# A two-layer hybrid decoder on one core: layers and expert bodies written out, one copy of the gathered tokens, a ninth weight buffer, norms applied by tile

## The chip, the core and the metric

The kernel runs on 1 of the cores of one Trainium2 chip. The metric is the device time of one execution in microseconds. The median of three runs of the kernel before is 1702.33 us (1701.65 to 1702.81).

## What is computed

The reference takes 256 tokens of 1024 float32 features through two layers. Each layer has three sub-layers, and each ends in x <- LayerNorm(alpha * x + f(x)).

```python
for l in range(2):
    mix = parallel_mixer(x, ...)      # short convolution and latent attention, gated, projected
    x = layer_norm(ALPHA * x + mix, ln1_g[l], ln1_b[l])
    xat = memory_cross_attention(x, mem, ...)          # 4 heads into 256 memory tokens
    x = layer_norm(ALPHA * x + xat, ln2_g[l], ln2_b[l])
    ffn = moe_ffn(x, ...)             # 64 experts, top 8 in 4 of 8 groups, plus a shared expert
    x = layer_norm(ALPHA * x + ffn, ln3_g[l], ln3_b[l])
```

An expert is silu(x @ w_gate) * (x @ w_up), times the token's gate, @ w_down, with inner width 256. Every expert's weights, 3 MB in float32, are read in every layer.

## The kernel before, in words

**Engines and order.** Each engine has its own program, written by hand, with semaphores between them. SyncE (SP) issues every weight load in one queue, in order; `alone` (L316) makes it wait for one semaphore and then go on, so what is behind a wait in its program waits too. TensorE, VectorE (DVE), ScalarE (ACT) and GpSimd (POOL) each run a loop `Fori(0, DEPTH)` over the two layers (L598, L769, L1201, L1479), with the counts they wait for worked out in registers from the layer and from `base`, the number of expert bodies already run. Only SyncE has the layers written out (L487).

**Dense part.** A layer has 24 weight loads of up to 2 MB (`LOADS`, L94), which go round the six slots of `ring`. Projections run as jobs through four PSUM banks `work` (L70 to L90). The layer begins with `xk0`, half of the projection of the memory tokens, then transposes XN (`xT0`) into XT with gain and bias of the norm applied on the way, then `cq`, `ckv`, `c`, `h` and so on. Only the transposed copy has gain and bias by then; X, in rows, is needed for the residual sum and gets them separately: GpSimd multiplies and adds for norms 1 and 2 (L627 to L638), both tiles of 128 tokens one after the other, once both are normalized, and then counts `ln_applied`. The gains and biases in rows are in `gb`, loaded by `load_ln` (L466).

**Norm 3.** The sum of the experts stands in the four PSUM banks `moe_sum`. `add_and_normalize(l, None, 2)` (L1392) takes statistics of both tiles, then multiplies the centred sums by the gain (`centred`, L1441), which needs `gb`, and then writes X (L1452). ScalarE writes XN (L1185); for tile 1 it waits for `centred_ready`, that is for the `centred` of tile 1 and so for the load. SyncE issues that load of ln3 for layer 0 behind the first six dense loads of layer 1 (L501 to L503), since `gb` shares its place with `xg_second`.

**Routing.** After norm 2, VectorE picks groups and experts in a chain of some 60 small instructions (L1637 to L1703), computes how many rounds of 32 slots the busiest expert needs (L1705 to L1713), and builds `sel`, the one-hot matrices of 8 experts (L1718). TensorE then gathers tokens as matmuls with `sel`, in a high and a low part: ScalarE rounds X to `x_hi` (L1299), GpSimd subtracts to get `x_lo` (L643). Before that TensorE does the shared expert's eight down products into `moe_sum` (L975) and counts `shared_down`, on which SyncE's load of unit 5 waits.

**Experts.** They run in 32 pairs of two. A pair has three units of 2 MB: expert 0's gate and up, expert 1's gate and up (for pairs "in halves", L372, the first and second half of both), and both down matrices. Units 0 to 7 lie in the six ring slots and two places of the arena (`ahead`, L237). Eight pairs are a body (24 units, so each place is used three times), and four bodies are a layer. SyncE loads unit m as soon as unit m - 8 has been read (`wait_unit_read`, L477): a down unit is free when the pair's down products are done, a gate and up unit when both are done, or its half for pairs in halves (the first three pairs of a layer, and the eighth of each body). On TensorE body 0 is written out (L1119) and bodies 1 to 3 are a loop (L1122 to L1124); SyncE has the same; ScalarE and VectorE loop over all four. Within a pair TensorE does gate and up (L1076), half of the previous pair's scatter into `moe_sum`, one gather matmul group for the next four pairs, the transposes of `hid`, the other half of the scatter, down (L1107) and another gather. Gathered tokens of one batch of four pairs lie in `xg_first`, those of the next in `xg_second` and `xg_more`.

## Time and profile before

| | us |
|---|---|
| median of three runs | 1702.33 |
| lowest and highest | 1701.65, 1702.81 |
| the profiled execution, time | 1701.95 |
| the profiled execution, first to last instruction (span) | 1700.1 |
| mean granted TensorE clock | 0.986 of full speed |
| busy: TensorE matmul, weight load | 1627.4, 907.1 |
| busy: VectorE, ScalarE, GpSimd | 430.8, 284.5, 71.0 |
| read from HBM | 507.64 MB, 299 GB/s over the span |

Times in the trace are counted from the span's start, and all reasoning is made on the profiled execution. Layer 0's experts run from about 384 to 842 us, layer 1's from about 1228 to 1687. Matmuls are pipelined, so a busy TensorE may still not be at its peak; the idle time in brackets behind a row, and what ended it, is what tells of a wait. "issue" there is a wait for nothing that the profile shows. SPq is SyncE's own queue; its rows are the times at which loads are issued, not those at which they land.

### The profile page before, as it was taken

What the parts mean: (1) busy time and instruction counts of PE and PEld (TensorE: products, weight loads), DVE (VectorE), ACT (ScalarE), POOL (GpSimd) and SP (SyncE); (2) the same over time, 40 slices, a digit from 0 to 9 for tenths busy, and PEclk for the clock granted to TensorE, in tenths of its full rate; (3) what the DMA queues carried; (4) which work ended last, traced back from release to release, by engine and by line L of the source; (5) the groups of instructions that cost most, each with busy time, mean ns of one, the idle gap of its engine ahead of it and who ended that gap; (6) DMA issues with size and microseconds to landing.
All of it is one profiled execution on the core that took longest, in us unless ns stands there. A gap on an engine that the chain in (4) does not pass through costs nothing.

```text
span 1700.1 us, 20631 instructions
## 1 busy us (share of the span) xinstructions
PE 1627.4 (96%) x8037; PEld 907.1 (53%) x8038; DVE 430.8 (25%) x893; ACT 284.5 (17%) x560; POOL 71.0 (4%) x88
## 2 busy tenths in 40 slices
PE   7999999999999999999789999999999999999996
PEld 5878867573333333333368787765733333333332
DVE  2122221162222222212222312112622222222223
ACT  1022011131111111111110320111311111111111
POOL 1000020030000000000000000200300000000000
PEclk9999999999999999999989999999999999999998
DMA  9246442468999999999950554434699999999995
GB/s 347 71 160 237 164 158 106 148 247 355 412 421 421 418 422 422 419 422 422 399 187 18 218 188 163 149 138 146 218 411 413 421 421 418 422 421 419 422 422 206
DMA packets 111222, 509.66 MB, mean 300 GB/s; under 512 B 8354, under 2 KB 12580, under 8 KB 68660
## 3 DMA queue, kind: packets, MB, share of 16 engines
q1 hardware_dynamic: 110592, 508.59, 75.2%
q8 instruction: 48, 0.79, 0.2%
q0 software_dynamic: 224, 0.12, 0.1%
q14 instruction: 18, 0.15, 0.0%
q10 hardware_dynamic: 340, 0.02, 0.0%
HBM read 507.64 MB, written 1.05 MB: 299 GB/s over the span
## 4 chain that ended last, share of the span: by engine, by line
PE 76%; DMA 11%; SPq 8%; DVE 3%; issue 1%; ACT 1%; DVEq 0%; ACTq 0%
PE work L686 37%; PE work L1076 20%; DMA ring<-in_w_up 9%; PE work L1107 9%; SPq L521 5%; PE work L987 3%; PE moe_sum L1030 3%; SPq L498 2%; DMA ring<-in_w_xk 1%; DMA arena<-in_ln_b 1%; PE work L1094 1%; PE moe_sum L1022 1%; PE work L994 0%; PE work L819 0%; DVE busiest L1708 0%
## 5 line engine op out<-in xcount | busy, mean ns | idle before, releaser
L1076 PE MATMUL work<-ring,arena 128*64 128x512 f32 x1216 | 288.6, 599 | 19.8 <-DMA ring<-in_w_up 13.6
L686 PE MATMUL work<-XT,ring 128*128 128x256 f32 (+1 forms) x1408 | 280.3, 360 | 1.3 <-DVE arena L1570 1.3
L686 PEld LDWEIGHTS work<-XT,ring 128*128 128x128 f32 x1408 | 247.5, 190 | 32.6 <-issue 3.0
L1076 PEld LDWEIGHTS work<-ring,arena 128*64 128x64 f32 x1216 | 90.1, 137 | 168.7 <-issue 156.7
L1107 PE MATMUL work<-ring,hidden 128*64 128x512 f32 x768 | 175.4, 598 | 1.0 <-DVE hidden L1769 1.0
L1776 DVE TENSOR_TENSOR out_lo<-work,out_hi 128x512 fp32r<-128x512 f32 x128 | 88.6, 692 | 231.1 <-ACT out_hi L1332 231.1
L686 PE MATMUL work<-ring,arena 128*128 128x512 f32 (+1 forms) x336 | 140.4, 577 | 0.0
L1765 DVE SCALAR_TENSOR_TENSOR hidden<-hidden,slot_gate,work 128x256 f32<-128x256 f32 x64 | 30.7, 480 | 419.1 <-ACT hidden L1328 419.1
L1332 ACT CAST out_hi<-work 128x512 fp32r<-128x512 f32 x128 | 75.1, 587 | 213.6 <-PE work L1107 213.6
L1328 ACT ACTIVATE hidden<-work 128x256 f32<-128x256 f32 x64 | 24.6, 385 | 491.7 <-PE work L1076 491.7
L1107 PEld LDWEIGHTS work<-ring,hidden 128*64 128x64 f32 x768 | 50.9, 136 | 100.4 <-issue 85.2
L686 PEld LDWEIGHTS work<-ring,arena 128*128 128x128 f32 x336 | 63.7, 190 | 71.7 <-issue 65.1
L987 PE MATMUL work<-sel,x_hi 128*128 128x256 f32 x288 | 91.7, 339 | 4.1 <-DVE sel L1718 3.7
L987 PEld LDWEIGHTS work<-sel,x_hi 128*128 128x128 f32 x288 | 55.7, 193 | 70.2 <-issue 63.2
L1076 PE MATMUL work<-arena 128*64 128x512 f32 x320 | 85.9, 596 | 7.1 <-DMA ring<-in_w_up 5.0
L1076 PE MATMUL work<-ring,xg_more 128*64 128x512 f32 x320 | 86.6, 592 | 0.0
L987 PE MATMUL work<-sel,x_lo 128*128 128x256 f32 x288 | 77.7, 291 | 0.0
L596 POOL TENSOR_TENSOR small<-small,minus_half 128x1 f32<-128x1 f32 x20 | 11.2, 559 | 1457.2 <-DVE small L1420 1454.4
L686 PE MATMUL work<-memT,ring 128*128 128x256 f32 x256 | 60.8, 402 | 10.1 <-issue 7.0
L1030 PE MATMUL moe_sum<-out_hi,selT 32*128 32x512 f32 x512 | 64.5, 494 | 1.8 <-DVE out_lo L1776 1.6
L686 PEld LDWEIGHTS work<-memT,ring 128*128 128x128 f32 x256 | 51.8, 203 | 19.3 <-issue 11.6
L1107 PE MATMUL work<-arena,hidden 128*64 128x512 f32 x256 | 58.5, 598 | 0.0
(227 smaller groups left out, 1424.7 us busy)
## 6 DMA issues: line engine op xcount, KB each, us to landing
ring<-in_w_gate SPq DMA_DIRECT2D x96, 1024.0 KB, 18.1
ring<-in_w_up SPq DMA_DIRECT2D x96, 1024.0 KB, 20.9
ring<-in_w_down SPq DMA_DIRECT2D x96, 1024.0 KB, 17.4
arena<-in_w_gate SPq DMA_DIRECT2D x32, 1024.0 KB, 20.5
arena<-in_w_up SPq DMA_DIRECT2D x32, 1024.0 KB, 22.3
arena<-in_w_down SPq DMA_DIRECT2D x32, 1024.0 KB, 17.8
ring<-in_w_in SPq DMA_DIRECT2D x28, 1024.0 KB, 12.7
ring<-in_w_xk SPq DMA_DIRECT2D x8, 1024.0 KB, 8.3
```

The lines of the kernel that those rows point to most:

```text
L498: sp.dma_start(dst, src).then_inc(slot_loaded[s], 16)
L521: sp.dma_start(dst, src).then_inc(slot_loaded[u], 16)
L686: mm = pe.matmul(dst, a, b, start=(k == 0), stop=(k == len(pairs) - 1))
L987: mm = pe.matmul(dst[:, :, t, :], part[:, t, c * P:(c + 1) * P], src, start=(part is x_hi), stop=(part is x_lo))
L1022: pe.matmul(moe_sum[i][:, :].rearrange("p (q c) -> p q c", c=KC), ident_r[:, :], rows, start=False, stop=False, skip_group_check=True)
L1030: mm = pe.matmul(moe_sum[2 * (q % TT) + half][:, :], selT[rows, b, k, :], part[rows, half * BANK:(half + 1) * BANK], start=False, stop=Fal ...
L1076: mm = pe.matmul(work[0][rows, :], xg[b][c][:, k * P + e * TT * SLOTS:k * P + (e + 1) * TT * SLOTS], w, start=(c == 0), stop=(c == KC - 1))
L1107: mm = pe.matmul(w[rows, :], hidT[:, c, rows], wd[:, e, c, half * BANK:(half + 1) * BANK], start=(c == 0), stop=(c == 1))
L1328: act.activation(hid, work[0][:, 0:EXPERT_DIM], ACT.Silu).then_inc(silu_ready, 1)
L1332: act.copy(out_hi[:, half * BANK:(half + 1) * BANK], work[1 + half][:, :]).then_inc(hi_ready[half], 1)
L1765: dve.scalar_tensor_tensor(out=hid, in0=hid, scalar=slot_gate[:, b, k:k + 1], in1=work[0][:, EXPERT_DIM:2 * EXPERT_DIM], op0=ALU.mult, op1 ...
L1776: dve.tensor_tensor(out_lo[:, cols], work[1 + half][:, :], out_hi[:, cols].bitcast(F32), ALU.subtract).then_inc(lo_ready[half], 1)
```

## The change

- The layer loops of all engines are written out, so layer 0's counts are constants. On TensorE and SyncE bodies 1 and 2 are written out too (only body 3 stays in the loop, with further rounds).
- `xg` is one buffer; the second batch of a body is kept in it in permuted blocks, so that it takes the blocks that the first batch has given up. `xg_more` goes. The room becomes `KEYS` (the cross-attention keys), and keys and `gb` together are a ninth unit, `EXTRA`. It holds unit 8 of each layer's first body and is used once a layer; its first half is loaded after the cross-attention scores, its second after norm 2 is applied.
- After that, places go round the old eight again (`place_of`), and the units wait for other predecessors (`wait_unit_read`).
- GpSimd applies norms by tile, and norm 3 of layer 0 too. ScalarE writes XN of layer 0's norm 3 without waiting for the gain; VectorE's `centred` steps stay only in layer 1, for tile 0.
- `load_ln` of ln3 is issued at the end of a layer's expert loads, ahead of the next layer's dense ones.
- `x_hi` is rounded by tile, `x_lo` follows, four of the shared expert's eight down products move in among the gathers, and the count of rounds moves behind the gathers.

```diff
+EXTRA = UNITS
...
-        xg_first, xg_second = view(2 * K, KC, BATCH * P), view(0, KC // 2, BATCH * P)
-        xg = [[xg_first[:, c, :] for c in range(KC)],
-              [(xg_second if c < KC // 2 else xg_more)[:, c % (KC // 2), :] for c in range(KC)]]
+        xg = view(2 * K, KC, BATCH, P)
+        def gathered(b, c):
+            return xg[:, c, :, :] if b == 0 else xg[:, c % 2::2, c // 2, :]
+        def gathered_pair(b, c, k):
+            return xg[:, c, k, :] if b == 0 else xg[:, 2 * k + c % 2, c // 2, :]
         ahead = view(6 * K, UNITS - RING, SLOT)
-        unit = [ring[:, u, :] if u < RING else ahead[:, u - RING, :] for u in range(UNITS)]
+        unit = [ring[:, u, :] if u < RING else ahead[:, u - RING, :] for u in range(UNITS)] + [arena[:, 0:SLOT]]
...
+        def place_of(m, first=False):
+            if not first:
+                return m % UNITS, m // UNITS + 1
+            return (m, 1) if m <= UNITS else ((m - UNITS - 1) % UNITS, (m - UNITS - 1) // UNITS + 2)
+        def units_used(u, l, body, first=False):
+            n = body * RING_USES
+            if u < RING:
+                return n + (l + 1) * DENSE_USES
+            if u == UNITS - 1:
+                return n + DEPTH - (l if first else l + 1)
+            return l if u == EXTRA else n
...
-            def wait_unit_read(m, pairs, halves, first=False):
-                q, part = divmod(m - UNITS, 3)
+            def wait_unit_read(m, pairs, halves, first=False, second=False):
+                if first:
+                    prev = m - UNITS - 1 if m <= 2 * UNITS else m - UNITS
+                elif second and m < UNITS:
+                    prev = m - (UNITS - 1) if m < UNITS - 1 else m - 2 * UNITS + 1
+                else:
+                    prev = m - UNITS
+                q, part = divmod(prev, 3)
                 if part == 2:
-                    alone(sp, down_filled[1], pairs + (q + 1))
+                    alone(sp, down_filled[1], snap(sp, pairs + (q + 1)))
                 else:
-                    alone(sp, gate_up_done, halves + (2 * q + (part if in_halves(q % BODY_PAIRS, first) else 1) + 1))
+                    late = part if in_halves(q % BODY_PAIRS, first or (second and q < 0)) else 1
+                    alone(sp, gate_up_done, snap(sp, halves + (2 * q + late + 1)))
...
-                    if l > 0 and n == RING - 1:
-                        alone(sp, gate_up_done, snap((base + 1) * (2 * BODY_PAIRS)))
-                        load_ln(l - 1, ln3_g, ln3_b, 2)
...
+                b, n = job("xscores", X_HEADS - 1)
+                alone(sp, filled[b], l * BANK_USES[b] + n)
+                load_unit(EXTRA, first[EXTRA // 3], True, (0,))
...
+                alone(sp, ln_applied, l * 3 + 3)
+                load_unit(EXTRA, first[EXTRA // 3], True, (1,))
...
+                load_body(base, first, range(EXTRA + 1, UNITS * RING_USES), True)
+                load_body(base + 1, firsts(1), range(UNITS * RING_USES), second=True)
+                load_body(base + 2, firsts(2), range(UNITS * RING_USES))
                 sp.reg_mov(more, 1)
-                sp.reg_mov(start, 1)
+                sp.reg_mov(start, 3)
...
+                alone(sp, down_filled[1], snap(sp, (base + 1) * BODY_PAIRS + (EXTRA // 3 + 1)))
+                load_ln(l, ln3_g, ln3_b, 2)
...
+                def root(which, t):
+                    alone(pool, moments_ready, l * 6 + (2 * which + t + 1))
+                    inverse_root(ln_rstd[:, t:t + 1], moments[:, 2 * t + 1:2 * t + 2], ln_rstd_ready)
+                def apply_norm(which, t):
+                    for half in range(2):
+                        pool.wait_ge(norm_ready[half], l * 6 + (2 * which + t + 3))
+                    pool.wait_ge(ln_loaded, (l * 3 + which + 1) * 32)
+                    step(pool.tensor_tensor(X[:, t, :], XN[:, t, :], gb[:, 0, :], ALU.mult))
+                    settle()
+                    ins = pool.tensor_tensor(X[:, t, :], X[:, t, :], gb[:, 1, :], ALU.add)
+                    if t == TT - 1:
+                        ins.then_inc(ln_applied, 1)
+                    elif which == 1:
+                        ins.then_inc(first_applied, 1)
+                    else:
+                        step(ins)
+                for which in range(2):
                     for t in range(TT):
+                        root(which, t)
+                        apply_norm(which, t)
+                for t in range(TT):
+                    pool.wait_ge(x_hi_ready, l * TT + (t + 1))
+                    pool.tensor_tensor(by_chunk(x_lo, t), in_chunks(X, t), by_chunk(x_hi, t).bitcast(F32),
+                                       ALU.subtract).then_inc(x_split_ready, 1)
+                for t in range(TT):
+                    root(2, t)
+                if l < DEPTH - 1:
                     for t in range(TT):
+                        apply_norm(2, t)
...
-            with pe.Fori(0, DEPTH) as l:
-                base = pe.value_load(bodies[0:1, bass.ds(l, 1)], min_val=0, max_val=4 * BODIES * DEPTH)
-                uses = pe.snap(base * RING_USES + l * DENSE_USES)
+            done = 0
+            for l in range(DEPTH):
+                base = done
+                seen.clear()
...
+                def add_shared(t, half, c):
+                    if half == 0 and c == 0:
+                        wait_job(l, "shared", t)
+                    return pe.matmul(moe_sum[2 * t + half][:, :], sharedT[:, c, t * P:(t + 1) * P],
+                                     w_down_sb[:, c, half * BANK:(half + 1) * BANK],
+                                     start=(c == 0), stop=False, skip_group_check=True)
+                shared_products = [(t, half, c) for t in range(TT) for half in range(2) for c in range(2)]
+                for t, half, c in shared_products[0:4]:
+                    add_shared(t, half, c)
...
+                    if c % 2 == 0:
+                        mm = add_shared(*shared_products[4 + c // 2])
+                        if c == KC - 2:
+                            mm.then_inc(shared_down, 1)
...
+                expert_body(snap(pe, base + 1))
+                expert_body(snap(pe, base + 2))
                 pe.reg_mov(more, 1)
-                pe.reg_mov(start, 1)
+                pe.reg_mov(start, 3)
...
-                        if t == 1:
-                            act.wait_ge(centred_ready, l + 1)
...
+                def round_input(t):
+                    act.copy(by_chunk(x_hi, t), in_chunks(X, t)).then_inc(x_hi_ready, 1)
+                normalize(l, 1, (0,))
+                tile_transposed(l, "xT2", 1, 0)
+                normalize(l, 1, (1,))
+                act.wait_ge(first_applied, l + 1)
+                round_input(0)
+                tile_transposed(l, "xT2", 1, 1)
                 w = wait_filled(act, l, "router")
                 take(act.activation(score, w[:, 0:TT * P].rearrange("p (t e) -> p t e", t=TT)[:, :, 0:EXPERTS], ACT.Sigmoid),
                      l, "router")
                 for t in range(TT):
+                    if t == 1:
+                        act.wait_ge(ln_applied, l * 3 + 3)
+                        round_input(1)
...
+                if l < DEPTH - 1:
+                    shift(0)
+                    shift(1)
+                    return
                 dve.wait_ge(ln_loaded, (l * 3 + 3) * 32)
                 settle()
-                for t in (1, 0):
-                    if t == 0:
-                        for half in range(2):
-                            dve.wait_ge(norm_ready[half], l * 6 + 7)
-                    for half in range(2):
-                        cols = slice(half * BANK, (half + 1) * BANK)
-                        ins = dve.scalar_tensor_tensor(out=centred[:, t, cols], in0=moe_sum[2 * t + half][:, :],
-                                                       scalar=moments[:, 2 * t:2 * t + 1], in1=gb[:, 0, cols],
-                                                       op0=ALU.subtract, op1=ALU.mult)
-                        if t == 1 and half == 1:
-                            tell(ins, centred_ready, l + 1)
-                            shift(1)
-                        else:
-                            step(ins)
+                for half in range(2):
+                    cols = slice(half * BANK, (half + 1) * BANK)
+                    step(dve.scalar_tensor_tensor(out=centred[:, cols], in0=moe_sum[half][:, :],
+                                                  scalar=moments[:, 0:1], in1=gb[:, 0, cols],
+                                                  op0=ALU.subtract, op1=ALU.mult))
+                shift(0)
+                shift(1)
                 settle()
-                for t in range(TT):
-                    dve.wait_ge(ln_rstd_ready, l * 6 + (5 + t))
-                    tell(dve.scalar_tensor_tensor(out=X[:, t, :], in0=centred[:, t, :], scalar=ln_rstd[:, t:t + 1],
-                                                  in1=gb[:, 1, :], op0=ALU.mult, op1=ALU.add),
-                         (layer_done if t == 0 else ln_applied), (l + 1 if t == 0 else l * 3 + 4))
+                tell(dve.scalar_tensor_tensor(out=X[:, 0, :], in0=centred, scalar=ln_rstd[:, 0:1],
+                                              in1=gb[:, 1, :], op0=ALU.mult, op1=ALU.add), layer_done, 1)
+                for half in range(2):
+                    cols = slice(half * BANK, (half + 1) * BANK)
+                    dve.wait_ge(norm_ready[half], l * 6 + 7)
+                    step(dve.tensor_tensor(X[:, 1, cols], XN[:, 1, cols], gb[:, 0, cols], ALU.mult))
+                settle()
+                tell(dve.tensor_tensor(X[:, 1, :], X[:, 1, :], gb[:, 1, :], ALU.add), ln_applied, l * 3 + 4)
...
+                then(dve.tensor_scalar(busiest[:, 1:2], busiest[:, 0:1], float(SLOTS), 1.0, ALU.is_gt, ALU.add))
+                for n in range(2, P // SLOTS):
+                    then(dve.tensor_scalar(busiest[:, 2:3], busiest[:, 0:1], float(n * SLOTS), None, ALU.is_gt))
+                    then(dve.tensor_tensor(busiest[:, 1:2], busiest[:, 1:2], busiest[:, 2:3], ALU.add))
+                step(dve.tensor_copy(rounds[:, l:l + 1], busiest[0:1, 1:2]))
+                then(dve.tensor_copy(bodies_f[:, 0:1], bodies[:, l:l + 1]))
+                then(dve.scalar_tensor_tensor(out=bodies_f[:, 1:2], in0=busiest[0:1, 1:2], scalar=float(BODIES),
+                                              in1=bodies_f[:, 0:1], op0=ALU.mult, op1=ALU.add))
+                tell(dve.tensor_copy(bodies[:, l + 1:l + 2], bodies_f[:, 1:2]), routing_ready, l + 1)
```

## Rows read from the trace of the kernel before

**Rows 1.** The page, 40 equal slices of the span: transfer rate.

```profile
GB/s 347 71 160 237 164 158 106 148 247 355 412 421 421 418 422 422 419 422 422 399 187 18 218 188 163 149 138 146 218 411 413 421 421 418 422 421 419 422 422 206
```

**Rows 2.** Windows: us, busy PE, PEld, DVE, ACT, POOL, clock, DMA share, GB/s.

```profile
420.00:500.00 80.00, 79.81 (x426) 30.33 (x420) 20.14 (x36) 13.08 (x25) 0.00 (x0) 1.00 1.01 416
...
450.00:460.00 10.00, 10.00 (x46) 3.27 (x42) 1.98 (x3) 1.11 (x2) 0.00 (x0) 1.00 0.99 390
...
845.00:850.00 5.00, 1.16 (x3) 0.99 (x4) 0.94 (x4) 1.45 (x2) 0.56 (x1) 0.50 1.05 384
```

**Rows 3.** Timeline of SyncE in the first body: start us, us, what.

```profile
387.79 0.80 SPq L521 DMA_DIRECT2D ring<-in_w_down  x2
...
432.32 0.80 SPq L521 DMA_DIRECT2D ring<-in_w_down  x2
...
475.17 0.81 SPq L521 DMA_DIRECT2D ring<-in_w_down  x2
```

**Rows 4.** L521, issue to landing, loads issued at 387.8 and 388.2.

```profile
DMA to landing us min/median/max: 4.8/5.8/6.9
```

**Rows 5.** The same, of those issued last at 418.5, 432.7 and 466.9.

```profile
DMA to landing us min/median/max: 10.6/11.7/12.7
...
DMA to landing us min/median/max: 6.4/7.4/8.5
...
DMA to landing us min/median/max: 13.1/14.6/16.1
```

**Rows 6.** Timeline of TensorE, first gate and up that waits for weights.

```profile
677.11 0.64 PE L1076 MATMUL work<-arena 128*64 128x512 f32 x1 [1.25 <-DMA ring<-in_w_up]
```

**Rows 7.** Timeline of TensorE, from layer 0 to layer 1.

```profile
848.84 16.04 PE L686 MATMUL work<-memT,ring 128*128 128x256 f32 x64 [7.00 <-issue]
868.97 1.20 PE L734 MATMUL work<-ident,arena 128*128 128x128 f32 x8 [4.10 <-ACT arena L1185]
...
876.21 18.99 PE L686 MATMUL work<-ring,XT 128*128 128x384 f32 x60 [0.85 <-DVE XT L1461]
```

**Rows 8.** Timeline of VectorE, from layer 0 to layer 1.

```profile
865.91 1.41 DVE L1441 SCALAR_TENSOR_TENSOR arena<-moe_sum,small,arena 128x512 f32<-128x512 f32 x2 [19.91 <-DMA arena<-in_ln_b]
...
874.83 0.18 DVE L1481 COPY par<-par_all 128x17 f32 x1 [3.60 <-issue]
```

**Rows 9.** L498, issue to landing, w_xk loads issued at 816.3 and 816.8.

```profile
DMA to landing us min/median/max: 17.6/19.0/20.4
```

**Rows 10.** Timeline of SyncE, from layer 0 to layer 1.

```profile
852.01 2.61 SPq L470 DMA_DIRECT2D arena<-in_ln_g  x1
```

**Rows 11.** The chain that ended last, first dense stages of both layers.

```profile
31.25 1.78 PE work L734 x16
33.04 45.85 PE work L686 x192
...
922.83 1.09 PE work L793 x10
```

**Rows 12.** Timeline of GpSimd, routing of layer 0.

```profile
353.14 4.67 POOL L631 TENSOR_TENSOR X<-arena 128x1024 f32<-128x1024 f32 x2 [1.21 <-ACT arena L1189]
357.89 4.80 POOL L634 TENSOR_TENSOR X<-X,arena 128x1024 f32<-128x1024 f32 x2
370.52 5.68 POOL L643 TENSOR_TENSOR x_lo<-X,x_hi 128x1024 fp32r<-128x1024 f32 x2 [7.83 <-ACT x_hi L1299]
```

**Rows 13.** Timeline of VectorE, routing of layer 0.

```profile
370.58 2.82 DVE L1708 TENSOR_TENSOR busiest<-busiest 128x1 f32<-128x1 f32 x1
...
376.51 0.69 DVE L1718 TENSOR_TENSOR sel<-pos,iota 128x512 fp32r<-128x512 f32 x1
```

**Rows 14.** Timeline of TensorE, routing of layer 0.

```profile
368.35 7.03 PE L975 MATMUL moe_sum<-ring,arena 128*128 128x512 f32 x16
377.26 0.39 PE L987 MATMUL work<-sel,x_hi 128*128 128x256 f32 x1 [1.87 <-DVE sel L1718]
...
384.03 7.09 PE L1076 MATMUL work<-ring,arena 128*64 128x512 f32 x32
```

142 lines of the change are left out of this document (51 added, 91 removed).

## Prediction

> **What bounds the kernel now.** I read the slices first: two layers of the same shape, in each a dense part of some 375 us in which DMA has room, then the experts, where the transfer rate stands at about 420 GB/s for some ten slices [rows 1]. The window from 420 to 500 says the same closer up: 416 GB/s at a full DMA share, while TensorE is at its upper clock, 2.4 GHz [rows 2]. A unit is 128 x 4096 floats, 2.10 MB, so at 421 GB/s one takes 4.98 us and the three of a pair 14.9 us. TensorE needs about 13.9 us for a pair: gate and up start at 384.0 [rows 14], and 21 pairs on TensorE is ready at 677.1 - 1.25 = 675.9 [rows 6]. Transfers are the slower side, so the lead that was loaded ahead melts, and from 677.1 on gate and up wait for their weights [rows 6]. The end of each expert part is therefore the landing of the last unit, not TensorE's work.
>
> The second bound is the passage between the layers. TensorE ends the last scatter at 848.84 - 7.00 = 841.8, starts the first projection of layer 1 at 848.8, finishes it at 864.9, and waits again: the transposes come at 869.0 and the first full run of `cq` at 876.2 [rows 7]. Two different things hold it. The 7.0 us ahead of 848.8 are labelled "issue"; the weights are not what is late, since the later of the two `w_xk` loads landed at 816.8 + 20.4 = 837.2 [rows 9]. Then VectorE sits 19.9 us [rows 8] until `ln_b` is there, because the last norm multiplies by it before tile 1 is let go, and after its two X writes another 3.6 us pass at the loop's end before L1481 [rows 8]. `ln_g` was issued only at 852.0, behind six dense loads [rows 10].
>
> Third, the 16 us of routing ahead of the experts, where VectorE's chain ends in `sel` at 376.5 and the first gather starts at 377.3 [rows 13, 14].
>
> **The passage (layers written out, load of ln3 ahead, XN straight from moe_sum).** The change lets ScalarE write XN of both tiles as soon as the shifts are there, without the load, and GpSimd applies gain and bias to X beside it. Removed: the 19.9 us wait, four `centred` instructions, two X writes and the way back to the loop's start. What is late next is the first projection itself. Steps after the last scatter's end E: about 0.5 us to fall through, 15.4 us for the 64 matmuls (it took 16.0 at a lower clock [rows 7]; the clock was 0.50 in the window before [rows 2], and I expect a shorter dip after a shorter idle), then 1.9 us to `cq`, a little over the 1.8 us that layer 0 shows from the start of the transposes at 31.25 to 33.04 [rows 11]. So `cq` at E + 17.8 instead of E + 34.4, that is 16.6 us. The run from there is warmer: 45.85 us in layer 0 against 876.21 to 922.83 = 46.6 in layer 1 [rows 11], 0.7 us more. **Sum 17.3 us.** GpSimd's four operations of 2.4 us each [rows 12] lie beside the projection; if that cover went they would delay only the residual, which is wanted at the mix sum more than 100 us on. The two ln3 loads now stand ahead of `w_xk`: 1 MB, 2.5 us at 421 GB/s, and I allow up to twice that again, since the wait for `ln_b` ended 13.9 us after `ln_g` was issued [rows 8, 10]; `w_xk` lands at 837.2 + 2.5 to 6.0 against a demand at 842.3, so at worst 0.9 us shows. Bounds of the passage: 10.3 us if the 7.0 us stay where they are, 19.5 if the projection runs at the full clock throughout and nothing is lost.
>
> The Trainium skill (Runtime: NRT & Kernel Launch, Instruction fetch mechanics) says that code is fetched ahead only in sequence and that a taken branch to a page not held stalls until it is fetched. By that rule the 7.0 us go, but the way back inside the expert loop would stall too, and writing out bodies would bring more. The trace agrees only with the first: the loop inside goes back near 607 and TensorE keeps its pace there. I give written-out bodies zero: no TensorE wait there names anything, and from pair 21 on the stage is bound by transfers anyway.
>
> **The routing.** Three edits go together. Norm 2 is applied by tile, so GpSimd's four operations (353.1 to 362.7 [rows 12]) become tile 0 in the idle time before and tile 1 at about 353.1 to 358.0; `x_hi` of tile 0 is rounded early, and the `x_lo` subtractions, 2.84 us each [rows 12], move from 370.5 to about 358 and 363.4. The count of rounds leaves the chain ahead of `sel`: eight small instructions, of which one took 2.8 us; from the end of L1703, some 0.7 us ahead of 370.6, to `sel` at 376.5 that is 6.6 us [rows 13]. TensorE puts four of eight shared products (16 matmuls 7.03 us [rows 14], so 3.5 us) in among the gathers.
> But the rows show why one was long: L1708 ended at 373.4 just as the first `x_lo` did, at 370.52 + 2.84 [rows 12, 13]. A VectorE operation with two SBUF inputs stood until GpSimd's was through. Moved to 363.4, the second `x_lo` stands across the group comparisons, which are such operations; I take 2.6 us of its 2.84 as lost there. Then `chosen` comes at 369.3 rather than 366.7, TensorE idles 1.4 us, places, does four products until 373.5; `sel` is there by 373.3. Gathers took 384.0 - 377.3 = 6.8 us [rows 14], in part at the lower clock; with 3.5 us of products among them and a warm clock about 8.9, so gate and up start at 382.4 instead of 384.0. **Gain 1.5 us per layer**, bounds -0.5 (the clock falls again) and +3.5 (no blocking).
> The Trainium skill (SBUF — State Buffer, Who interferes with whom) states this as an exclusive lock held for a whole instruction and counts plain VectorE copies and scalar operations in 2-port modes in as well. By it more of the router's chain would stand and the gain would be near zero; by the row alone it is what I took.
>
> **The ninth buffer.** On its face it lets 2.1 MB more be loaded before the experts start, 5.0 us at 421 GB/s off the end of a stage bound by transfers. I went through who frees what. The unit is used once per layer, so unit m of the first body takes the place of m - 9 only up to 16; from 17 it waits for m - 8 as before, and in the second body units 0 to 6 wait for m - 7, one *less* ahead. Times of before: a load issued into an empty queue at 387.8 landed 6.9 us after its second half's issue at 388.2, 7.4 us after release [rows 3, 4]. Before, unit 8 landed at 395.1 and unit 17, released at 432.3, landed 8.5 us after 432.7, at 441.2 [rows 3, 5]. With the change unit 9 lands at 395.1 and unit 16 as unit 15 did, at 418.5 + 12.7 = 431.2 [rows 5], and the next is not released until gate and up of pair 3 end at 432.2: it lands at 439.6. Of 5.0 us 1.6 are left. Then unit 25: before it was released at 466.3 and landed at 466.9 + 16.1 = 483.0 [rows 5]. Now it waits for unit 18, read when pair 6's gate and up end at 475.1 (the release after which `w_down` was issued at 475.2 [rows 3]), and lands at 482.5. **Gain 0.5 us per layer**; bounds -1.3 (before, 390 GB/s between 450 and 460 [rows 2] delayed unit 25 by about 1.8 us over the even pace; a like dip behind the new waits would come on top) and +1.6. What is behind SP's waits then is the rest of the queue: each bubble moves every later unit.
> The last shared product, and with it the sixth unit's load, comes later by about 5 us; the queue is empty then, and unit 9 is released only 4 us after the start, so this costs nothing.
>
> **The rest.** One copy of the gathered tokens: the same copies and matmuls at other addresses, none added; a block is overwritten after the pair that reads it, in TensorE's own order. Zero; a few tenths if strided copies are slower, hidden under gate and up. End of layer 1: two `centred` instructions (0.7 us each [rows 8]) and an X write are exchanged for two half products and one sum of the same widths; +0.1 us.
>
> **Sum.** 17.3 + 2 x (1.5 + 0.5) - 0.1 = 21.2 us off the profiled execution's 1701.95 (span 1700.1 and 1.85 around it) gives 1680.8; the median is 0.4 above that execution, so **1681 us**.
>
> **Rivals.** *The ninth buffer pays in full* and the router is not blocked: 5.0 instead of 0.5 and up to 3.5 instead of 1.5 per layer; with the first alone 1681 - 9 = 1672. For it speaks that the stage is bound by transfers; against it the release times, which are rules of the code. 0.1. *The passage keeps its issue stall*, because TensorE fetches its next code under a full queue either way: 7 us back, 1688. For it: nothing shows that the branch alone is guilty. Against: the scatter after the inner loop's end started with no such stall. 0.2. *Cold code in the written-out bodies* makes it slower: two more bodies per layer run once each, fetched while transfers are at 420 GB/s; each stall would be of the passage's size, 7.0 us. It decides from four unhidden stalls on, 28 us against the 21 gained, which is 1681 + 28 = 1709; with two in each of the four such bodies it is 1681 + 56 = 1737. Against it: the first body of before ran once, was written out, and shows no stall. 0.03. My forecast 0.6; what is left, 0.07, is mixtures between.
>
> **The numbers.** The range takes the passage at 15 to 19.5, the routing and buffer bounds partly offsetting each other, and reaches to the rival at 1688: 1673 to 1689. A measurement tells about 0.2%, 3.4 us, from no change: faster 0.95, within it 0.02, slower 0.03.
>
> **What would show it.** Right: no wait for `ln_b`; the projection of layer 1 starting within 2 us of the last scatter, `cq` 17 to 19 us after it; `sel` near 373 with a long VectorE instruction in the comparisons; the first gate and up near 382; a hole in the transfer rate near 430 and 473, and the wait for weights beginning about pair 20 as before. Wrong: an "issue" of 7 us at the passage, an unbroken rate from 388 on with the expert part 5 us shorter, or holes in TensorE in the second and third bodies.

## The result, and the profile after

The changed kernel takes **1680.26 us** (median of 4 runs, 1679.52 to 1683.15) against 1701.99 for the kernel before on the same chip: a ratio of 0.9875, 95% interval 0.9862 to 0.9889. The profiled execution has a span of 1677.7 us against 1700.1. Cut at the same five points of TensorE's timeline in both traces, the 22.4 us between the spans lie as follows (us; S is the start of the first gate and up, E the end of the last scatter, cq the first full run behind the transposes):

```
part                              before   after   gained  predicted
layer 0 up to S                   384.0    380.7     3.4     1.5
experts of layer 0, S to E        457.8    460.3    -2.5     0.5
passage, E to cq of layer 1        34.4     15.7    18.7    16.6
layer 1, cq to S                  352.2    348.1     4.1     2.2
experts of layer 1                458.9    460.6    -1.7     0.5
behind the last scatter            12.8     12.4     0.4    -0.1
```

(2.2 is 1.5 for the routing and 0.7 for the warmer run.) The total came out as forecast (1681 us), but two terms were too small, and the expert part, where I forecast a small gain, got longer. The slices still show two layers bound by transfers at 421 GB/s; the page's line:

```profile
GB/s 347 75 149 252 143 156 135 176 226 373 372 407 421 418 421 421 418 421 421 410 301 0 289 162 126 165 142 176 276 385 394 421 421 419 421 421 419 421 421 216
```

**The passage.** TensorE's timeline, where [rows 7] had 7.00 us of issue ahead of the projection and 4.10 behind it:

```profile
839.41 0.50 PE L1082 MATMUL moe_sum<-out_hi,selT 32*128 32x512 f32 x4 [0.82 <-DVE out_lo L1836]
...
840.56 0.40 PE L1082 MATMUL moe_sum<-out_lo,selT 32*128 32x512 f32 x4
840.89 14.08 PE L728 MATMUL work<-memT,ring 128*128 128x256 f32 x64
854.80 1.94 PE L777 MATMUL work<-ident,arena 128*128 128x128 f32 x16
856.66 13.71 PE L728 MATMUL work<-ring,XT 128*128 128x384 f32 x45
```

No gap is left. The projection starts as the scatter ends, and takes 13.9 us (840.89 to 854.80) because the clock never left its upper level (granted clock 1.00 in the stretches from 840 to 850 and from 850 to 860).

**The routing.** VectorE and GpSimd, where [rows 12, 13] had the blocked L1708 and `sel` at 376.5:

```profile
357.69 2.80 DVE L1702 TENSOR_TENSOR arena<-arena,iota 128x64 f32<-128x64 f32 x1
...
363.23 2.87 DVE L1721 TENSOR_TENSOR arena<-small 128x64 f32<-128x64 f32 x1
...
371.93 0.69 DVE L1767 TENSOR_TENSOR sel<-pos,iota 128x512 fp32r<-128x512 f32 x1
```

```profile
357.56 2.86 POOL L680 TENSOR_TENSOR x_lo<-X,x_hi 128x1024 fp32r<-128x1024 f32 x1
363.11 2.91 POOL L680 TENSOR_TENSOR x_lo<-X,x_hi 128x1024 fp32r<-128x1024 f32 x1 [2.70 <-ACT x_hi L1340]
```

Each VectorE instruction of 2.8 us ends within 0.1 us of a GpSimd subtraction (360.49 and 360.42; 366.10 and 366.02). The second stands in the group comparisons, as forecast; the first, on L1702, is one that the forecast didn't have. TensorE gathers from 372.76 and starts gate and up at 380.65: 7.9 us with four shared products among them, where I had 8.9.

**The transfers behind the ninth unit.** Three rows of the table by stretches (engines, granted clock, DMA share, GB/s), then SyncE's issues:

```profile
420.00:430.00 10.00, 9.81 (x56) 4.00 (x53) 2.83 (x6) 1.55 (x3) 0.00 (x0) 1.00 0.78 310
...
450.00:460.00 10.00, 10.00 (x58) 3.87 (x60) 1.68 (x4) 0.97 (x2) 0.00 (x0) 1.00 1.01 358
...
470.00:480.00 10.00, 10.00 (x58) 4.12 (x56) 3.47 (x7) 2.73 (x5) 0.00 (x0) 1.00 0.90 360
```

```profile
414.76 0.33 SPq L548 DMA_DIRECT2D arena<-in_w_gate  x1
415.13 0.43 SPq L548 DMA_DIRECT2D arena<-in_w_up  x1
428.94 0.80 SPq L548 DMA_DIRECT2D ring<-in_w_down  x2
...
463.32 0.42 SPq L548 DMA_DIRECT2D ring<-in_w_up  x1
471.73 0.33 SPq L548 DMA_DIRECT2D ring<-in_w_gate  x1
```

These are the two holes of the forecast: nothing is issued from 415.6 to 428.94 (before, [rows 2] had 416 GB/s from 420 to 500 at a full share), and again from 463.7 to 471.73. The share falls to 0.78 and 0.90, and what had been loaded ahead is mostly spent again.

### The profile page after: what moved, and what is told of

Its sections match the earlier page's. It is cut to its first block, busy times and chain, and to the rows that moved or that the text cites. A ratio compares the mean times of both kernels' runs of the same rounds, so it can differ in the third digit from the quotient of the medians.

```text
span 1677.7 us, 19829 instructions
## 1 busy us (share of the span) xinstructions
PE 1618.2 (96%) x8037; PEld 901.8 (54%) x8037; DVE 423.4 (25%) x886; ACT 280.5 (17%) x555; POOL 80.5 (5%) x92
## 4 chain that ended last, share of the span: by engine, by line
PE 79%; DMA 12%; SPq 5%; DVE 3%; issue 1%; ACT 1%; DVEq 0%
PE work L728 38%; PE work L1128 20%; DMA ring<-in_w_up 11%; PE work L1159 9%; SPq L548 5%; PE moe_sum L1082 3%; PE work L1035 3%; PE moe_sum L1021 1%; DMA ring<-in_w_xk 1%; PE work L1146 1%; PE moe_sum L1074 1%; PE work L1042 0%; PE work L777 0%; PE work L864 0%; DVE arena L1721 0%
## 5 line engine op out<-in xcount | busy, mean ns | idle before, releaser
L1128 PE MATMUL work<-ring,arena 128*64 128x512 f32 x1536 | 365.5, 599 | 19.6 <-DMA ring<-in_w_up 12.4
L1128 PEld LDWEIGHTS work<-ring,arena 128*64 128x64 f32 x1536 | 118.4, 137 | 206.8 <-issue 194.7
L1128 PE MATMUL work<-arena 128*64 128x512 f32 x512 | 136.6, 598 | 10.0 <-DMA ring<-in_w_up 7.4
L1128 PEld LDWEIGHTS work<-arena 128*64 128x64 f32 x512 | 42.4, 137 | 92.4 <-issue 84.5
L1082 PEld LDWEIGHTS moe_sum<-out_hi,selT 32*128 32x128 f32 x512 | 24.5, 181 | 60.8 <-issue 52.3
```

The costliest lines, as they stand in the source:

```text
L1082: mm = pe.matmul(moe_sum[2 * (q % TT) + half][:, :], selT[rows, b, k, :], part[rows, half * BANK:(half + 1) * BANK], start=False, stop=Fal ...
L1128: mm = pe.matmul(work[0][rows, :], gathered_pair(b, c, k)[:, rows], w, start=(c == 0), stop=(c == KC - 1))
```

## The experiments

Each is an edit of the changed kernel. e3 to e7 and e10 ran once each, e1, e2 and e9 four times, e8 and e11 five times; where a kernel ran more than once the time is the median. The cuts above are made in one trace of each (us):

```
run                                   S      experts 0  passage  cq to S  experts 1
before                                384.0  457.8      34.4     352.2    458.9
changed                               380.7  460.3      15.7     348.1    460.6
e1  no ninth unit                     379.5  462.3      15.7     348.1    460.8
e2  ninth unit rotates                379.0  455.4      15.7     348.1    455.5
e3  TensorE's layer loop back         381.0  460.4      25.9     348.0    460.5
e4  XN waits, load late               379.6  461.1      29.5     348.6    460.4
e5  shared products first             382.2  460.2      15.7     349.8    460.3
e6  bodies in the loop                380.5  458.9      15.7     348.1    459.0
e7  XN waits, load early              380.9  460.4      15.7     348.1    461.0
e8  ninth rotates, tables early       380.6  455.1      15.7     347.8    455.6
e9  no ninth, bodies in the loop      379.2  458.8      15.7     348.1    459.7
e10 as e9, shared products first      381.8  458.3      15.7     349.8    459.2
e11 as e8, first subtraction early    378.5  455.7      15.7     347.0    455.8
```

S of layer 0 lies up to 2 us apart in kernels that do the same work up to there (e2 and e7), and SyncE's issues near 310 us are already apart by 1.7 (e2 and the changed kernel); `cq` to S of layer 1 agrees within 0.1 us in six kernels. So sizes of the routing are read in layer 1.

**e1, without the ninth unit.**

```
-            return (m, 1) if m <= UNITS else ((m - UNITS - 1) % UNITS, (m - UNITS - 1) // UNITS + 2)
+            return m % UNITS, m // UNITS + 1
...
-                if first:
-                    prev = m - UNITS - 1 if m <= 2 * UNITS else m - UNITS
-                elif second and m < UNITS:
-                    prev = m - (UNITS - 1) if m < UNITS - 1 else m - 2 * UNITS + 1
-                else:
-                    prev = m - UNITS
+                prev = m - UNITS
```

> The changed kernel with the ninth unit taken out: unit m waits for m - 8 throughout, nothing else differs. Theory A (who frees what decides, and a unit used once a layer costs more at its two seams than it gives): from the first gate and up to the last scatter layer 0 takes 457.8 us and layer 1 458.9 as in the kernel before, against 460.3 and 460.6 in the changed one, no hole in the transfer rate near 420 to 430 and 470 to 480; total some 4 us below the changed kernel, 1676. Theory B (a unit more ahead pays its 5.0 us per layer even if used once): the expert parts grow by about 5 us each, total 1690.

Measured: 1680.35 us (1679.54 to 1681.15, ratio 0.987, interval 0.985 to 0.989), no difference from the changed kernel. The holes are gone: 419 GB/s at a share of 1.01 between 420 and 430. The expert parts take 462.3 and 460.8 us, so by this pair the ninth unit, used once, brings 2.0 and 0.2; in layer 0 this trace has slices of granted clock 0.83 from 720 to 730 and from 790 to 800, which the changed kernel's has not, and one such pair's first half took 8.78 us against 7.09. Both figures of the expectation were missed. The ninth unit is no loss, but as used it is worth little, and the longer expert part is not its doing.

**e2, the ninth unit in rotation for three bodies** (unit m waits for m - 9 up to the end of the third body).

```
+            g = i * UNITS * RING_USES + m
+            return g % (UNITS + 1), g // (UNITS + 1) + 1
...
+                prev = m - UNITS if i is None else m - UNITS - 1
```

> The changed kernel with the ninth unit kept in the round for the three bodies that are written out: unit m goes to place m mod 9 and waits for m - 9 (72 units, eight turns of nine); the fourth body goes round eight. Theory A: no wait of the queue is late any more, so the whole lead of 2.10 MB is kept and each expert part is 5.0 us shorter than with eight units: 452.8 and 453.9 us, 7.5 us less than in the changed kernel; total 1665 to 1668, and an unbroken 420 GB/s from 390 on. Theory B (the lead is lost to something else, such as the halves' smaller rows or TensorE's own pace): expert parts stay within 2 us of the changed kernel's and the total within 4 us of 1680.

Measured: 1669.65 us (1667.97 to 1671.07), ratio 0.981, interval 0.979 to 0.983: faster than the kernel before and, by intervals that don't touch, than the changed one; some 2 us above what theory A gave. The stretch with the first hole is full:

```profile
420.00:430.00 10.00, 9.90 (x58) 3.94 (x60) 2.63 (x6) 1.02 (x3) 0.00 (x0) 1.00 1.01 419
```

and the expert parts take 455.4 and 455.5 us, 4.9 and 5.1 less than the changed kernel's: a unit's transfer is 5.0 us. Against e1, which has no ninth unit, it is 6.9 and 5.3. The same buffer pays in full when the wait distance stays at nine for three bodies, and hardly at all when it falls back to eight in the first. The fourth body of e2 falls back to eight too, and loses nothing: its queue moves 419 to 423 GB/s in every stretch from 700 to 800, and TensorE waits for weights from 713.80 on, so that by then places come free as fast as they are filled.

**e3, TensorE's layer loop back.**

```
-            for l in range(DEPTH):
-                base = done
-                seen.clear()
+            with pe.Fori(0, DEPTH) as l:
+                base = pe.value_load(bodies[0:1, bass.ds(l, 1)], min_val=0, max_val=4 * BODIES * DEPTH)
```

> The changed kernel, with only TensorE's layer loop put back as a loop (the base is read from memory again at its head); loads, norms and bodies as in the changed kernel. Theory A (the 7.0 us of issue are the way back of TensorE's loop): an idle time labelled issue of 6 to 8 us is back between the last scatter of layer 0 and the first projection of layer 1, cq comes about 8 us later than in the changed kernel (a lower clock on top), total 1687 to 1689. Theory B (the stall was due to the full transfer queue or to the wait for the load of the norm): no such stall, total within 2 us of 1680.

Measured: 1689.89 us, span 1688.0, that is 10.3 over the changed kernel's. The timeline:

```profile
840.91 0.40 PE L1079 MATMUL moe_sum<-out_lo,selT 32*128 32x512 f32 x4
849.70 12.54 PE L728 MATMUL work<-memT,ring 128*128 128x256 f32 x49 [8.39 <-issue]
```

8.39 us of issue are back. The projection then takes 15.6 us instead of 13.9; the table by stretches has a granted clock of 0.65 in the idle time and still 0.84 behind it, where the changed kernel has 1.00 in both:

```profile
840.00:850.00 10.00, 1.54 (x17) 0.67 (x14) 3.94 (x13) 2.79 (x4) 3.74 (x4) 0.65 1.06 382
850.00:860.00 10.00, 10.00 (x40) 8.53 (x40) 0.00 (x0) 0.59 (x1) 6.70 (x3) 0.84 1.04 383
```

Of the difference in span 8.4 + 1.7 is all but 0.2. What else rides on the loop (VectorE, ScalarE, SyncE written out) stayed, so the stall is TensorE's own way back. The queue that brings instructions has two packets in it from 842 to 850, of 16 KB each, where the changed kernel has none:

```profile
q8 instruction: 2, 0.03, 2.6%
```

The edit also brings back the read of `base` at the loop's head. No run takes it apart, but a read of the same kind (`done`) stands in every kernel ahead of the last scatter, where TensorE idles some 0.8 us in all, so it can be no large part of 8.39. The Trainium skill (Runtime: NRT & Kernel Launch, Instruction fetch mechanics) has a stall wherever a taken branch leads outside what is held; by that rule the trace agrees here.

**e4 and e7, XN waits for ln3's load**, which is issued behind the dense loads (e4) or in its new early place (e7).

```
                     if which == 2:
+                        if l == 0:
+                            act.wait_ge(ln_loaded, (l * 3 + 3) * 32)
                         for half in range(2):
```

> The changed kernel with the ln3 load of layer 0 put back behind the first six dense loads of layer 1, and ScalarE made to wait for it before it writes XN of the last norm of layer 0. All else as changed. Theory A (the old order made the projection's successor wait for that load): the load lands near 862, the transposes start at about 864 instead of 854.8, total 9 to 10 us above the changed kernel, 1689 to 1690. Theory B (the passage was bound by something else once the loop is gone): total within 2 us of 1680.

> The changed kernel, but ScalarE waits for the load of ln3's gain and bias of layer 0 before it writes XN, with the load in its new early place. Theory A: the place of the load alone brought the 13.7 us by which the run with the late load and the same wait was longer; 1679 to 1681.5 us, no gap ahead of the transposes. Rival B: the wait costs something by itself, because the load, though issued near 815, lands only behind other transfers: transposes later than 855.5, up to 1690 us.

Measured: 1693.25 us for e4, 1680.33 for e7. In e4 ScalarE, then TensorE:

```profile
863.78 2.78 ACT L1242 ACTIVATE arena<-moe_sum,small 128x512 f32<-128x512 f32 x4 [25.54 <-DMA arena<-in_ln_b]
```

```profile
866.67 3.65 PE L780 MATMUL work<-ident,arena 128*128 128x128 f32 x16 [12.00 <-ACT arena L1242]
```

SyncE issued `ln_g` at 849.20 there; the passage is 13.8 us longer: 12.0 us of waiting for the load, and most of the rest is that the transposes behind it run at the lower clock (granted clock 0.50 from 866 to 871) and take 3.4 us instead of 1.9. In e7 the same wait shows no gap. So of the two edits that took VectorE's 19.9 us [rows 8] off the chain, the load's place alone would have done for XN. That XN without the wait would have done with the late load is likely, since only X then needs the load, but no run has it. The change made both.

**e5, the eight shared products ahead of the gathers again.** By then five traces (before, changed, e1, e3, e4) had E of layer 0 at 841.3 +- 0.6 us, wherever S lay (the sixth, e2's, has 834.4), and I took the later load of the sixth unit for the cause.

```
-                for t, half, c in shared_products[0:4]:
-                    add_shared(t, half, c)
+                for t, half, c in shared_products:
+                    mm = add_shared(t, half, c)
+                mm.then_inc(shared_down, 1)
...
-                    if c % 2 == 0:
-                        mm = add_shared(*shared_products[4 + c // 2])
-                        if c == KC - 2:
-                            mm.then_inc(shared_down, 1)
```

> The changed kernel with all eight products of the shared expert ahead of the gathers again, as in the kernel before (the change puts four of them among the gathers). Theory A, formed on the last scatter's end, which stays at 841.3 +- 0.6 us in six traces while the first gate and up start anywhere from 379.5 to 384.0: the load of the sixth unit waits for the last of those products, so moving them delayed the transfers (issued at 380.33 instead of 375.48) and ate most of what the routing gained. Then this kernel starts gate and up about 2 us later (382.5 to 383.3), issues that load near 376, and the last scatter of layer 0 still ends at 840.5 to 842: about 1680.5 us. Rival B, what I predicted: the later load costs nothing, and the expert part lasts 460.3 from wherever it starts: each layer 2.2 us later, last scatter at 843.1, about 1684.7 us.

Measured: 1682.37 us, between the two. The load is issued at 376.31 and S is 382.16, but E moves with S: the expert parts are 460.2 and 460.3 us. Theory A fell, and the constant E was a coincidence of terms. My reading, which no further run tests: behind a hole everything is timed from the release that ends it, and that goes with S.

**e6, TensorE's second and third bodies in the loop.**

```
-                expert_body(snap(pe, base + 1))
-                expert_body(snap(pe, base + 2))
                 pe.reg_mov(more, 1)
-                pe.reg_mov(start, 3)
+                pe.reg_mov(start, 1)
```

> The changed kernel with TensorE's second and third expert bodies back in the inner loop; layers stay written out. Theory A: writing out bodies brought nothing, since TensorE's way back inside the loop shows no gap while 7.0 to 8.4 us were lost at the layer loop's: 1679 to 1681.5 us. Rival B: each way back costs what the layer loop's does and the transfers hide only part: two more per layer at up to 8.4 us, 1687 us or more, and a TensorE gap labelled issue at the start of the second and third body.

Measured: **1676.37 us, faster** than either theory had it; span 3.1 less than the changed kernel's, 1.4 and 1.6 in the two expert parts. TensorE at pair 20 and 21, first of the changed kernel, then of e6:

```profile
659.75 7.09 PE L1128 MATMUL work<-ring,arena 128*64 128x512 f32 x32 [1.13 <-issue]
676.03 0.61 PE L1128 MATMUL work<-arena 128*64 128x512 f32 x1 [2.68 <-DMA ring<-in_w_up]
```

```profile
659.66 7.09 PE L1128 MATMUL work<-ring,arena 128*64 128x512 f32 x32 [1.22 <-issue]
674.53 0.64 PE L1128 MATMUL work<-arena 128*64 128x512 f32 x1 [1.26 <-DMA ring<-in_w_up]
```

TensorE itself doesn't stall on new code; its weights land 1.4 us later. The clock is no rival in layer 0: both traces have a granted clock of 1.00 in every stretch of 20 us from 380 to 840. The DMA queues of the stretch from 600 to 800 (packets, MB, share of 16 engines), first of the changed kernel, then of e6:

```profile
q1 hardware_dynamic: 12039, 83.93, 101.1%
q8 instruction: 8, 0.13, 0.3%
```

```profile
q1 hardware_dynamic: 12083, 84.24, 101.4%
```

The third and fourth body of the changed kernel bring in 8 packets of instructions, and the weights move 0.31 MB less in the same 200 us, 0.7 us at 421 GB/s. That is half of the 1.4; the other half is not accounted for. e6 fetches no such packet there, nor does the kernel before. Over the span it is 65 packets against 45 (48 before).

**e9 and e10: the same without the ninth unit**, e10 with the shared products first as well. The diffs are those of e1, e6 and e5 together.

> The changed kernel without the ninth unit and with TensorE's second and third bodies back in the loop, so both edits of two earlier runs at once. Theory A: written-out bodies cost about 1.5 us per layer, because each body that runs as new code fetches its instructions through the same DMA engines as the weights (8 more packets of instructions between 600 and 800 us, 9 between 1300 and 1660, and pair 21 is ready 1.4 us later), and that is independent of the ninth unit: 1680.35 - 3.9 = 1676.5 us, 45 packets of instructions instead of 65, first expert part of layer 1 some 459.3 us instead of 460.8. Rival B: the 3.9 us of that one run was chance, or came with the ninth unit's holes: 1680 us.

> As the run before, and besides all eight products of the shared expert ahead of the gathers, as in the kernel before. Theory A: without the ninth unit there are no holes in the transfers behind, so here the load of the sixth unit (issued near 376 instead of 380) counts: gate and up start 1.7 us later per layer, but the expert part is 1.3 to 1.7 us shorter, 457.8 to 458.2 us in layer 1, and the time is that of the run before within 1 us: 1676 to 1677.5. Rival B: the load's place costs nothing here either, the expert part stays at 459.3, and the time is 3.4 us longer: 1680 us.

Measured: e9 1676.37 us (1675.73 to 1676.94, ratio 0.9854, interval 0.9838 to 0.9871), where e1 had 1680.35; 45 packets of instructions against e1's 65. The expert parts are 3.5 and 1.1 us shorter than e1's. The expectation's figure holds, and the slowest of e9's four executions is 2.6 us under the fastest of e1's; they ran on different chips, and the intervals of their ratios overlap a little (e1's begins at 0.985). With e6 beside it I take the effect for real, at 1.4 to 2.0 us per layer. e10: 1679.06 us. Its expert parts are 458.3 and 459.2, only 0.5 shorter than e9's, against S 1.7 us later per layer: if the early load counts, then for 0.5 and not 1.5, and like kernels differ by nearly as much (layer 1 of e7 and of the changed kernel by 0.4). Here the rival was the nearer one.

**e8 and e11, the router's chain**, both on e2. e8 makes `ones` and `before_group` ahead of norm 2; e11 also moves the first subtraction into GpSimd's idle time:

```
                 for which in range(2):
                     for t in range(TT):
+                        if which == 1 and t == 1:
+                            split_input(0)
                         root(which, t)
```

> The kernel with the ninth unit in rotation, and besides VectorE makes the two constant tables of the routing (ones, before_group) before it normalizes for norm 2, not in the router's chain, where the changed kernel shows a 2.80 us instruction standing until GpSimd's subtraction ends. Theory A: the chain shortens by about 1.1 us per layer (it ends next in the one-by-one instructions behind the same subtraction), sel, the gathers and the sixth unit's load come 1.1 us sooner: gate and up at 377.9, last scatters 1.1 us sooner per layer, 1667.4 us. Rival B: the end of the expert part is set by transfers whose start does not move with the chain, or the next two-input instruction stands in its place: as the ninth unit alone, 1669.6 us.

> The ninth unit in rotation and the tables made early, as in an earlier run, and besides ScalarE rounds tile 0 of the input before it normalizes tile 1, and GpSimd subtracts there, in its idle time near 347, instead of at 357.7, where VectorE's first instruction of the router's chain stood 1.33 us instead of 0.28. Theory A: two-input VectorE instructions stand while GpSimd works, so the chain gets 1.05 us shorter per layer: that instruction 0.28 us, sel near 370.8, and 1669.3 - 2.1 = 1667.2 us. The second subtraction still blocks one for 2.8 us. Rival B: the chain is then held by something else (ScalarE's sigmoid, or rounding tile 0 delays tile 1's norm): 1669.3 us or more.

Measured: e8 1669.04 us (ratio 0.9799, interval 0.9783 to 0.9815), no difference from e2: the next two-input instruction, L1705, stood 1.33 us in the place of L1702, which is its rival B; `cq` to S of layer 1 is 0.3 us shorter. e11 1667.78 us (ratio 0.9803, interval 0.9789 to 0.9817): that instruction takes 0.29 us and `cq` to S is 347.0, 0.8 to 0.9 less than in e8, as far as it can be read in a trace; the ratios of e2, e8 and e11 can't be told apart. VectorE and GpSimd in e11:

```profile
358.24 0.29 DVE L1711 TENSOR_TENSOR arena<-arena,par 128x128 f32<-128x128 f32 x1 [2.51 <-ACT arena L1353]
...
362.16 2.85 DVE L1729 TENSOR_SCALAR penalty<-small 128x16 f32<-128x16 f32 x1
```

```profile
346.03 2.85 POOL L673 TENSOR_TENSOR x_lo<-X,x_hi 128x1024 fp32r<-128x1024 f32 x1 [4.06 <-ACT x_hi L1343]
...
362.13 2.85 POOL L673 TENSOR_TENSOR x_lo<-X,x_hi 128x1024 fp32r<-128x1024 f32 x1 [5.54 <-ACT x_hi L1343]
```

This time a scalar operation with one SBUF input, which takes 0.17 us elsewhere, stood 2.85 us, until GpSimd was through at 364.98.

## Why the prediction was right, and where it was not

**The passage: mechanism right, 2 us too small.** The 7.0 us of issue went with the layer loop (e3 brings back 8.4), and the wait for `ln_b` went with the load (e4 brings back 13.8). `cq` came at E + 15.7, not E + 17.8. The step that was mis-sized is the projection: I kept most of its 16.0 us at the lower clock, expecting a shorter dip; with no idle time there is no dip and it takes 13.9. The other 0.5 is the fall-through, which costs nothing visible. Behind it the transposes take the 1.9 us that I had. The rival that the stall stays, at 0.2, is refuted.

**The routing: 1.5 forecast, 3.4 measured in layer 1** (4.1 less the warmer run's 0.7), just below my upper bound, though my reason for that bound was wrong: the second subtraction did block VectorE, for 2.6 us as taken. `sel` came at 371.9, not 373.3, and the gathers with their products took 7.9 us at the upper clock instead of 8.9. Moving four products is worth 1.7 of it (e9 against e10, e5 against the changed kernel). The remaining 1.7 are the split of norm 2 and the round count taken off the chain, which no run takes apart. The forecast also read the blocking too narrowly. It named one instruction that stood, L1708. The trace of before has more: L1653 stood until GpSimd's second addition was through (362.69), and L1711 until its second subtraction was (376.20):

```profile
361.73 1.00 DVE L1653 TENSOR_TENSOR small<-arena 128x16 f32<-128x16 f32 x1
...
374.09 2.12 DVE L1711 SCALAR_TENSOR_TENSOR bodies_f<-busiest,bodies_f 1x1 f32<-1x1 f32 x1
```

So both subtractions stood in VectorE's way before, and both do after, on L1702 and L1721; the change moved that cost and did not remove it. e11 takes the first one off, and with the tables made early that is worth 1.1 us in layer 1 (348.1 in e2, 347.0 in e11). The Trainium skill (SBUF — State Buffer, Who interferes with whom) counts scalar operations in a 2-port mode among those that stand while GpSimd works, and I went by the row, that is by two-input instructions; e11's `TENSOR_SCALAR` of 2.85 us agrees with the page. The consequence that I had drawn from it, a gain near zero, did not come: the gain was above both figures.

**The expert part: the term that failed.** I forecast 0.5 us less per layer with a lower bound of 1.3 more; it got 2.5 and 1.7 us longer. Four runs make a path from the kernel before to the changed one (expert parts of layer 0 and 1):

```
before                                     457.8  458.9
e10: all but what stands below             458.3  459.2   +0.5 +0.3
e9:  shared products among the gathers     458.8  459.7   +0.5 +0.5
e6:  ninth unit, used once per layer       458.9  459.0   +0.1 -0.7
changed: bodies written out on TensorE     460.3  460.6   +1.4 +1.6
```

So the ninth unit's term was small, as forecast (0.3 on the mean of two layers, 0.5 forecast; 1.1 by e1, which has the clock slices), though differences of this size can't be told from those between like kernels. Its reason was right too: the holes lie where the release times put them, and e2, which keeps the distance, gets the 5 us that my first rival gave to the unit on its face. Used as the change uses it, the release rules of the code decide, as the prediction had it. The step that failed is one that I gave nothing. "I give written-out bodies zero" missed 1.5 us per layer (e6 against the changed kernel): I looked for stalls of TensorE, found none in the second body, and didn't ask where the code comes from. It comes by DMA, in a stage where my own first paragraph says that transfers are the slower side. A second step that I gave nothing may have failed too: "the queue is empty then", of the sixth unit's later load, missed 0.5 by e9 against e10, but 0.1 and 0.3 by the changed kernel against e5. That, and the +0.5 and +0.3 of e10, which stay unexplained, are the size of the differences between like kernels.

The rule on branches that the prediction cites was right about the layer loop, and by it the way back inside the expert loop would stall too. The traces speak against that: with the bodies looped there is no packet of instructions from 600 to 800 us, and no gap that the changed kernel doesn't have. That writing out costs transfers, not stalls, is what e6 and e9 show; that the packets share an engine with the weights, and so delay one sixteenth of each landing, would explain why 0.13 MB of code displaces 0.31 MB of weights, but it is only argued.

**The sum** was right in part by luck: 2.1 more on the passage, 3.8 more on two routings and 0.5 more behind the last scatter made up for 5.2 lost in two expert parts. The total alone hides that.

## What to carry to other kernels

In a stage bound by transfers, an added buffer is worth its load time only if the waits behind it keep the longer distance until the consumer itself waits for the transfers; where the rotation falls back earlier, the queue runs empty for what was gained. In such a stage written-out code is fetched beside the weights and is not free, so write out the loop whose way back shows a stall, and keep the loop whose way back shows none. Before believing a total, cut both traces at the same points and compare part by part.

## What the hardware showed that was not expected

- Two bodies of code that run for the first time cost 1.4 to 1.6 us per layer (e6), without a gap labelled issue on the engine that runs them beyond what the looped bodies show: the packets of 16 KB (0.13 MB in 8) come through the DMA engines, and the pair's weights land 1.4 us later.
- TensorE's way back to the top of the layer loop costs 7.0 us before and 8.4 us in e3; its way back inside the expert loop costs nothing that a row shows. Writing out two bodies in each of two layers adds 20 packets, so a body is about five, some 80 KB; a layer of before is about 24 (half of its 48). Both are estimates from the counts of packets.
- A VectorE operation on 128 x 16 elements with one SBUF input stood 2.85 us while GpSimd subtracted, beside the two-input ones. Moving the first subtraction to idle time freed one; the second found something to block in each of the traces of before, the changed kernel, e8 and e11.
- Loads issued into an empty queue didn't make up for the wait: unit 25, released at 471.7 and issued beside the next unit, landed 8.6 us after the release (472.11 + 8.2), where I had taken 7.4 from [rows 4]. Counted from S that is 0.7 us later than before (99.7 against 99.0), where the forecast had it 0.5 earlier.
